# Ten weight slots, TensorE's expert pairs written out, and fillers ahead of a router's ranks

## The reference, cut to what matters

```python
xt = rmsnorm_2(x, norm2_g).reshape(T, D)                     # T = 512, D = 1024
g_logits = xt @ w_rg + b_rg;  g_idx = argmax(g_logits)       # 4 groups
e_in = (xt @ w_re + b_re).reshape(T, 4, 8)[group g_idx]      # 8 experts of the group
top_v, top_i = top_k(e_in, 2)
top_w = softmax(top_v) * softmax(g_logits)[g_idx]
# for each expert e, on the tokens xb that chose it:
ys = (silu(xb @ w_gate[e]) * (xb @ w_up[e])) @ w_down[e]     # 1024 -> 512 -> 1024
y[token] += top_w * ys
x = x + y
```

## Time and profile before

| | us |
|---|---|
| median of 3 runs | 1706.51 (1705.78 to 1707.2) |
| the profiled execution | 1707.3 |
| its span, first to last instruction | 1705.6 |
| TensorE busy in it | 1667.4 |
| VectorE busy | 807.9 |
| ScalarE busy | 321.3 |

### The profile page before, as it was taken

The page is one execution under the profiler, slowest core; times in us unless marked ns, Lnnn a source line. Parts: engine busy times, 40 slices in busy tenths (PEclk is TensorE's granted clock), DMA queues, the critical chain, the costliest instruction groups (busy, mean ns, idle before and its releaser), DMA issues.

```text
span 1705.6 us, 19789 instructions
## 1 busy us (share of the span) xinstructions
PE 1667.4 (98%) x7794; PEld 1044.1 (61%) x7794; DVE 807.9 (47%) x1762; ACT 321.3 (19%) x678; POOL 18.7 (1%) x39
## 2 busy tenths in 40 slices
PE   8999999999999999999999999999899999999998
PEld 4455544588888888878444455547754545454452
DVE  4973558587777772364895233335521211111123
ACT  1121334311111100120334244300200000000000
POOL 0001000000000000000000000000000000000001
PEclk9999999999999999999999999999999999999999
DMA  9976020012221213141211110533499999999998
GB/s 402 373 272 210 18 99 1 35 50 99 99 90 58 83 69 136 50 163 56 99 50 50 50 50 0 197 113 134 162 407 428 429 429 430 427 429 429 428 428 337
DMA packets 30247, 335.60 MB, mean 197 GB/s; under 512 B 3209, under 2 KB 5785, under 8 KB 10593
## 3 DMA queue, kind: packets, MB, share of 16 engines
q1 hardware_dynamic: 22464, 310.56, 44.7%
q10 hardware_dynamic: 5168, 14.91, 2.3%
q0 software_dynamic: 2544, 9.18, 1.5%
HBM read 319.66 MB, written 18.37 MB: 198 GB/s over the span
## 4 chain that ended last, share of the span: by engine, by line
PE 84%; DMA 7%; DVE 5%; ACT 2%; issue 1%; SPq 0%; ACTq 0%; DVEq 0%
PE bank L1497 16%; PE bank L1067 16%; PE bank L1115 8%; PE bank L1262 6%; PE bank L1506 5%; DMA pool<-in_w_expert_up 4%; PE bank L871 3%; PE bank L1270 3%; PE bank L1442 3%; PE bank L1184 3%; PE bank L1237 3%; PE bank L657 2%; DMA arena<-in_w_expert_up 2%; DMA pool<-in_w_ada 2%; PE bank L861 2%; PE bank L1039 2%
## 5 line engine op out<-in xcount | busy, mean ns | idle before, releaser
L1497 PE MATMUL bank<-pool,arena 128*64 128x512 f32 x1216 | 334.6, 594 | 7.3 <-DMA arena<-in_w_expert_up 3.8
L1067 PE MATMUL bank<-pool 128*128 128x256 f32 x1232 | 266.1, 379 | 0.8 <-ACT pool L2634 0.8
L1067 PEld LDWEIGHTS bank<-pool 128*128 128x128 f32 x1232 | 234.3, 190 | 32.4 <-issue 1.0
L1497 PEld LDWEIGHTS bank<-pool,arena 128*64 128x64 f32 x1216 | 107.6, 137 | 173.4 <-issue 164.3
L2550 DVE TENSOR_TENSOR arena<-arena,bank 128x512 f32<-128x512 f32 x16 | 11.0, 688 | 279.0 <-PE bank L1497 279.0
L1506 PEld LDWEIGHTS bank<-arena 128*128 128x128 f32 x960 | 109.5, 192 | 12.2 <-issue 12.2
L1262 PE MATMUL bank<-pool 128*128 128x512 f32 x256 | 114.5, 595 | 0.0
L1506 PE MATMUL bank<-arena 128*128 128x128 f32 x960 | 113.6, 277 | 0.0
L1262 PEld LDWEIGHTS bank<-pool 128*128 128x128 f32 x256 | 47.5, 190 | 55.3 <-issue 54.2
L1497 PE MATMUL bank<-xT,arena 128*64 128x512 f32 x160 | 70.6, 594 | 3.6 <-DMA pool<-in_w_expert_up 3.6
L1497 PE MATMUL bank<-arena 128*64 128x512 f32 x160 | 70.4, 593 | 0.0
(11 more groups left out here) (432 smaller groups left out, 2230.4 us busy)
## 6 DMA issues: line engine op xcount, KB each, us to landing
pool<-in_w_expert_gate SPq DMA_DIRECT2D x27, 2048.0 KB, 25.7
pool<-in_w_expert_down SPq DMA_DIRECT2D x27, 2048.0 KB, 28.0
pool<-in_w_expert_up SPq DMA_DIRECT2D x22, 2048.0 KB, 25.0
pool<-in_w_in SPq DMA_DIRECT2D x15, 2048.0 KB, 8.5
pool<-in_w_ada SPq DMA_DIRECT2D x12, 2048.0 KB, 18.8
pool<-in_w_up SPq DMA_DIRECT2D x11, 2048.0 KB, 8.1
arena<-in_w_expert_gate SPq DMA_DIRECT2D x5, 2048.0 KB, 29.8
xT<-in_w_expert_up SPq DMA_DIRECT2D x5, 2048.0 KB, 24.8
```

What stands on the lines that cost most here:

```text
L1067: ins = pe.matmul(up_quarter(u, p), lhs[:, k, :], rhs[:, k, :], start=(k == 0), stop=(k == 3))
L1497: ins = pe.matmul(dst[b * CAP:(b + 1) * CAP, :], lhs(b, k), rhs(b, k), start=(k == 0), stop=(k == n_k - 1))
```

## The change

- **A tenth slot.** `arena[:, 12800:16896]` becomes slot 9. Slab 9 (up of expert 3) is loaded into it once the first rows are transposed (`xk_full` at 1), ahead of `ring8` in SyncE's list. Slab c goes to slot c modulo 10; the use of slab c releases the load of slab c + 10. SyncE's list is a loop of two rounds over 30 loads and 26 loads written out: 86 in all, where there were 87.
- **Room for it.** The router's tables leave that part of `arena`: they go to 11264 to 12800, into `block1` and into `mn`. The squares get eight buffers in the new slot's place. `wpick` becomes `pick`, and `wpT` becomes `pickb`; so the weighted picks are made behind pair 14 instead of ahead of it.
- **TensorE's pairs** 1 to 15 are written out, with no loop.
- **Overflow blocks** on all four engines: block 0, then a `Fori` from 1 with an `If` inside.
- **Fillers**: `kept_warm(8, 5)` behind the transposes 0 to 5 and ahead of the wait for `oh_rdy`.
- Two semaphores used once each on ScalarE (`cact_rdy`, `e1_rdy`) become one, `ac_first`.

```diff
-        sqr = [view(arena, (11776, 12288, 12800, 15936, 12288, 12800, 15936, 12288)[m], T) for m in range(KD)]
+        sqr = [view(arena, 12800 + m * T, T) for m in range(KD)]
-        wpick = view(arena, 9728, NT, P)
-        pickO = (view(arena, 9728, NT, CAP), view(arena, 9984, NT, CAP))
-        xsO = view(arena, 15936, KD, CAP)
-        wpT = view(arena, 15936, NT, P)
+        wpick = pick
+        pickO = (view(arena, 8192, NT, CAP), view(arena, 8448, NT, CAP))
+        xsO = view(arena, 8704, KD, CAP)
+        wpT = pickb
-        xsT = view(arena, 10240, KD, P)
-        sg = view(arena, 11264, EF)
-        hE = view(arena, 11776, EF)
-        ysb = view(arena, 12288, D)
+        xsT = view(arena, 9728, KD, P)
+        sg = view(arena, 10752, EF)
+        hE = view(arena, 11264, EF)
+        ysb = view(arena, 11776, D)
-        ws += [arena[:, SLOT:2 * SLOT], hT.rearrange("p k t -> p (k t)"), xT.rearrange("p k t -> p (k t)")]
+        ws += [arena[:, SLOT:2 * SLOT], hT.rearrange("p k t -> p (k t)"), xT.rearrange("p k t -> p (k t)"), arena[:, 12800:16896]]
...
-        landed = [sem(f"landed{i}") for i in range(9)]
+        landed = [sem(f"landed{i}") for i in range(10)]
-        loads = [0] * 9
+        loads = [0] * 10
...
+
+        def tables(base, r_at, end, *shapes):
+            for name, shape in shapes:
+                R[name] = view(base, r_at, *shape)
+                r_at += int(np.prod(shape))
+            assert r_at <= end, r_at
+
+        tables(arena, 11264, 11776, ("t2", (2, NT * E)), ("cm", (E, 7)))
+        tables(arena, 11776, 12800, ("io", (E,)), ("r4", (4,)), ("g7", (7,)), ("bs", (E,)), ("ohs", (NT + 1, E)), ("lg", (NT, 36)),
+               ("gs", (NT, 4)), ("g1", (NT, 4)), ("gm", (NT,)), ("gx", (NT,)), ("em", (NT, E)), ("top", (NT, 8)), ("ix", (NT, 8)),
+               ("d", (NT,)), ("oh", (2, NT * E)), ("nb", (E,)), ("adj", (E,)), ("rk", (2, NT)), ("rb", (2, NT)), ("big", (2, NT)))
+        tables(block1, 0, P, ("cin", (E,)), ("be", (2, E)), ("bx", (2,)), ("ge", (NT, 4)), ("pg", (NT,)), ("w1", (NT,)), ("ed", (NT,)))
+        mn = sb("mn", [P, 2 * P])
+        tables(mn, 36, P, ("sl", (2, NT)), ("slo", (2, NT)))
+        tables(mn, P, 2 * P, ("row", (P,)))
...
-        turn9 = (0, 3, 1, 4, 2, 5, 6, 7, 8)
+        turn10 = (0, 3, 1, 4, 2, 5, 6, 7, 8, 9)
...
                 load(("eu", 1), 4, up_of(1))
+                load("ring9", 9, up_of(3), (S["xk_full"], 1))
                 load("ring8", 8, up_of(2), (S["xk_full"], 2 * NT))
                 sp.wait_ge(S["ov_step"], 1)
...
 
-                    used, of = ("g_full", "uu_full", "yy_full")[r % 6 // 2], (gate_of, up_of, down_of)[(r + 9) % 6 // 2]
-                    at = turn9[r % 9]
-                    sp.wait_ge(S[used], i * 3 + (r // 6 + 1))
-                    sp.dma_start(ws[at][:, :], of(i * 6 + (2 * ((r + 9) // 6) + (r + 9) % 2)))\
-                      .then_inc(landed[at], 16)
-
-                with sp.Fori(0, 4) as i:
-                    for r in range(18):
+                    used, of = ("g_full", "uu_full", "yy_full")[r % 6 // 2], (gate_of, up_of, down_of)[(r + 10) % 6 // 2]
+                    at = turn10[r % 10]
+                    sp.wait_ge(S[used], i * 5 + (r // 6 + 1))
+                    sp.dma_start(ws[at][:, :], of(i * 10 + (2 * ((r + 10) // 6) + r % 2))).then_inc(landed[at], 16)
+
+                with sp.Fori(0, 2) as i:
+                    for r in range(30):
                         next_slab(i, r)
-                for r in range(15):
-                    next_slab(4, r)
+                for r in range(26):
+                    next_slab(2, r)
                 for t in range(NT):
                     sp.wait_ge(S["comb"], LAST.index((t, 1)) + 1)
...
                     rows_of(x)
+                kept_warm(8, 5)
                 pe.wait_ge(S["oh_rdy"], 1)
                 pe.matmul(bank[3][:, 0:(NT + 1) * E], tris[:, :], R["ohs"].rearrange("p t e -> p (t e)"), start=True, stop=False)
                 for t in range(NT):
...
-                base += [16] * 3
+                base += [16] * 4
 
                 def placed(i, c):
 
-                    at = turn9[c % 9]
-                    return at, i * 32 + (base[at] + 16 * (c // 9))
+                    at = turn10[c % 10]
+                    return at, i * 48 + (base[at] + 16 * (c // 10))
 
                 def both_k(n_k, lhs, rhs, dst, later=None):
 
...
-                def block_of(i, n_more, least):
-
-                    with pe.If(n_more > least):
-                        pe.wait_ge(S["ov_step"], i * OVS + 2)
-                        if i == 0:
-                            n_more = pe.value_load(smi[0:1, 42:43], min_val=0, max_val=OVB)
-                            pe.wait_ge(S["xt_ev"], 2)
...
-                        ins.then_inc(S["ov_step"], 1)
-                        if i + 1 < OVB:
-                            block_of(i + 1, n_more, i + 1)
-                        if i == 0:
-                            pe.wait_ge(S["ov_back"], 48)
-
-                block_of(0, most, CAP)
+                def block_of(i):
+
+                    pe.wait_ge(S["ov_step"], i * OVS + 2)
+                    if isinstance(i, int):
+                        pe.wait_ge(S["xt_ev"], 2)
+                    for k in range(KD):
...
+                    for half in range(2):
+                        ins = full_k(0, lambda k: hET[:, k, 0:CAP], lambda k: w[:, k, half * 512:(half + 1) * 512], n_k=4,
+                                     sl=bank[6 + half][0:CAP, :])
+                    ins.then_inc(S["ov_step"], 1)
+
+                with pe.If(most > CAP):
+                    block_of(0)
+                    n_more = pe.value_load(smi[0:1, 42:43], min_val=0, max_val=OVB)
+                    with pe.Fori(1, OVB) as i:
+                        with pe.If(n_more > i):
+                            block_of(i)
+                    pe.wait_ge(S["ov_back"], 48)
                 pair(0, [placed(0, c) for c in range(6)], first=True)
-                with pe.Fori(0, 4) as i:
-                    for q in range(1, 4):
-                        pair(i * 3 + q, [placed(i, 6 * q + c) for c in range(6)])
-                for p in range(13, E // 2):
+                for p in range(1, E // 2):
                     pair(p, [placed(0, 6 * p + c) for c in range(6)], last=(p == E // 2 - 1))
 
                 pe.wait_ge(S["xt_ev"], E + 1)
...
 
-                def picks(i, weighted=False):
-
+                def picks(i, last=False):
 
...
                     ve.tensor_tensor(pick, pick, pickb, ALU.add).then_inc(S["pick_rdy"], 1)
-                    if weighted:
-                        ve.wait_ge(S["pick_rdy"], i + NT)
-                        for t in range(NT):
-                            for b, dst_ in enumerate((wpick, pickb)):
-                                ins = ve.tensor_scalar(dst_[:, t, :], R["row"], R["sl"][:, b, t:t + 1], wt[:, b, t:t + 1],
-                                                       ALU.is_equal, ALU.mult)
-                        ins.then_inc(S["pick_part"], 1)
-                        ve.wait_ge(S["pick_part"], i * 2 + 1)
-                        ve.tensor_tensor(wpick, wpick, pickb, ALU.add).then_inc(S["pick_rdy"], 1)
+                    if last:
                         return
                     ve.tensor_scalar(R["sl"], R["sl"], float(-P), None, ALU.add).then_inc(S["pick_part"], 1)
                     ve.wait_ge(S["pick_part"], i * 2 + 1)
                     ve.wait_ge(S["pick_rdy"], i + NT)
+
+                def weights_placed(i):
+
+                    ve.wait_ge(S["pick_rdy"], i + NT)
+                    for t in range(NT):
+                        for b, dst_ in enumerate((wpick, pickb)):
+                            ins = ve.tensor_scalar(dst_[:, t, :], R["row"], R["sl"][:, b, t:t + 1], wt[:, b, t:t + 1],
+                                                   ALU.is_equal, ALU.mult)
+                    ins.then_inc(S["pick_part"], 1)
+                    ve.wait_ge(S["pick_part"], i * 2 + 1)
+                    ve.tensor_tensor(wpick, wpick, pickb, ALU.add).then_inc(S["pick_rdy"], 1)
 
             if on("end"):
                 n2 = col("norm2", 0, 8)
...
                     pair(p, False, False)
                     picks(p + 2)
                 pair(E // 2 - 3, False, False)
-                picks(E // 2 - 1, weighted=True)
+                picks(E // 2 - 1, last=True)
                 pair(E // 2 - 2, False, False)
+                weights_placed(E // 2 - 1)
                 pair(E // 2 - 1, False, True)
                 ve.wait_ge(gath[0], 64)
                 for t in range(2):
```

More of the change, by code:

```diff
@@ L408, in two_blocks @@
         rs1 = view(upper, 7168, 512)
-        mn = sb("mn", [P, 2 * P])
         mnf, mnb = mn[:, 0:P], mn[:, P:2 * P]
@@ L1601, in _ @@
-                block_of(0, most, CAP)
+                def block_of(i):
[4 more added lines that the diff above has]
+                        for t in range(NT):
```

(45 more changed lines are left out.)

123 lines of the change are left out of this document (35 added, 88 removed).

## The result

The changed kernel takes 1710.36 us (median of 9 runs, 1707.74 to 1712.11), beside 1706.62 for the kernel before in the same comparison (9 runs, 1705.29 to 1708.79): a ratio of 1.0019, 95% interval 1.0010 to 1.0028. Forecast were 1699.5 and a range up to 1702.6. It is slower, by 0.2%, where 0.4% faster was forecast. The profiled execution took 1711.37 us, 4.1 more than its counterpart of before.

The account below looks back on a forecast made before the run. TensorE and DMA were both taken as at their limit, DMA pacing the last pairs. Slot -5.1, fillers -2.4 and fetches +0.5 made -7.0 us, from a median of 1706.5 to 1699.5; range 1697.0 to 1702.6.

Parts of the forecast that it names:

- The jump over the overflow blocks: TensorE's jump ahead of pair 0, over two blocks instead of fifteen: nothing, bounds a gain of 1.2 and a loss of 1.5.
- One more such gap: Loss bound of the jump ahead of pair 0: another idle gap of TensorE like the present one, 1.5 us.
- The fetches of the written-out pairs: Expert stage: 13 instruction fetches of 16 KB added to a full DMA stream, 0.5 us lost by bytes.
- The rival with one DMA engine: Expert stage: one of 16 DMA engines carries all added fetches, 7.9 us instead of 0.5, time 1706.9; chance 0.05.
- The row taken against it: Chain of waits before the change: pairs 10 to 12 without a fetch take 61.12 us, 12 to 14 with two 61.18.
- The tenth slot: Expert stage: each awaited slab lands one place earlier in the DMA stream, 5.1 us gained, bounds 4.9 and 6.1.
- The fillers: Router, ahead of the ranks: eight fillers keep TensorE's clock at full, so the expert stage starts 2.4 us earlier.
- The loop's jump back: TensorE's loop over pairs, between pairs 3 and 4: costs nothing, 28.53 us across it, so writing out saves nothing there.
- slot, clock, fetches, jump: The forecast's bounds: slot 4.9 to 6.1, clock (by the fillers) 1.8 to 2.9, fetches 0.4 to 1, jump either way.

Follow-up runs that it names:

- c_early: c_fixed with the tenth slot's slab requested as the router works, ahead of ring8: 1705.08 us, ratio 0.9994 to the kernel before.
- c_fixed: Changed kernel's layout and fillers, loops of the kernel before; tenth slot filled once, with slab 78, behind pair 0's first matmul: 1701.81 us, ratio 0.9968.
- a_late9: Changed kernel with slab 9 requested when pair 0's first matmul has run, not as the router works: 1703.73 us, ratio 0.9985.
- b_flat: Kernel before with only TensorE's pairs 1 to 15 written out, nine slots, no fillers: 1711.07 us, ratio 1.0026.
- c_nofill: c_fixed without the eight fillers: 1702.47 us, ratio 0.9975 to the kernel before.
- b_fill: Kernel before with only the eight fillers added ahead of the wait for the ranks' input: 1705.87 us, ratio 0.9993.
- a_nofill: Changed kernel without the eight fillers ahead of the ranks: 1709.39 us, ratio 1.0011 to the kernel before.
- a_late9_loop5: a_late9 with TensorE's pairs 1 to 10 as two rounds of a five-pair loop, 11 to 15 written out: 1704.49 us, ratio 0.9986.

## Why the prediction was wrong

**The jump over the overflow blocks** is the step that failed first. It was priced at nothing, with a loss of at most 1.5, although the text named what happens: ring8 and ring9 in flight when the target is fetched. It measured 5.7 us at the start of pair 0 (2.7 of gap, 3.0 of matmuls at the lower level behind it). c_early against c_fixed shows it with one load moved, a_late9 against the changed kernel as well; and that the code is what TensorE waits for is shown by the instruction packet, 1.52 to 1.61 us ahead of pair 0 in every kernel and late only where the tenth slot's slab is in flight. "One more such gap" was the wrong bound: the packet is as late as the slabs take to drain, and the clock comes on top. The text's own numbers could have priced it. By an estimate from them, four slabs at 4.89 us, the first issued at 1203.52, are in the queues until 1223.1 at the earliest, and the gathering ahead of the jump was forecast to end at 1222.4. The text asked of the fourth slab only whether it delays the first reload, at 1233.61.

**The fetches of the written-out pairs** are the second. Priced at 0.5 by bytes, they measured 4.5 us in b_flat (14.7 against 10.2 lost; 3.2 of a later slab, 1.3 of clock behind it) and 4.3 us in the median. The rival with one DMA engine (7.9) had the right mechanism, slabs land with the slowest engine, and the wrong distribution: the distance of the first engine from the last grows from 2.3 to 5.7 us. Its price was low besides: a packet takes about 1.0 us of its engine and not 0.61 (five were 0.3% of 16 engines over 105 us). That the setbacks fall on several engines is an estimate: twelve of 1.0 us on one would be 12 us, and the distance grew by 3.3. Which engine took which fetch isn't shown. The row taken against it, 61.18 against 61.12 us, had two fetches in it, and those may fall on engines that are ahead. Two of thirteen was no sample.

**The tenth slot** did what the text said. The cleanest comparison is c_nofill with the kernel before, both with the loop of three pairs and without fillers: 6.2 us lost against 10.2, and 3.9 us in the medians, for a slab worth 4.1 there. b_flat loses 14.7 us, a_late9, which adds the slot, 9.6: 5.1 less, as priced, though the two differ in more than the slot. The changed kernel has 11.1 lost where 5.1 were forecast: 4.5 are the fetches, and the other 1.5 are more of the same, since the slab that pair 14 awaits is 6.8 us from first to last write there, 5.5 in a_late9, and lands 1.3 us later, counted from pair 0's mark. Why the engines are further apart than in a_late9 stays open.

**The fillers** gave 2.1 us of the 2.4 in the profile. In the medians they are worth 0.9 (b_fill) and 0.7 (c_nofill to c_fixed), neither clear of nothing; and in the changed kernel nothing is left of them at the mark of pair 0, and the median without them (a_nofill) is 1.0 lower. The hole ahead of the ranks is not the only place where the clock falls.

**The loop's jump back** at nothing held for the body of three pairs. The rule of the Trainium skill ("Runtime: NRT & Kernel Launch", section on instruction fetch), that a taken branch stalls when its target isn't in the current window of two pages, is not borne out there: the body of three pairs ran on without a packet or a stall. At the body of five pairs (2.4 us) and at the jump over the overflow blocks the trace agrees with it.

**The range.** The bounds given with it (slot, clock, fetches, jump), taken all at once, make 1696.7 to 1702.3 and not 1697.2 to 1701.5. The measured time is outside both, so this isn't the step that failed.

The gain forecast was thus made, by 5.1 of the slot and 2.1 of the fillers, and given back twice, 5.7 at the jump and 4.5 by the fetches: 3.0 us slower. With the other 1.5 at pair 14's slab, 0.3 ahead of the router and -0.6 in the tail these are the 4.1 between the two profiled executions, to 0.1; the medians differ by 3.7.

## What to carry to other kernels

When DMA bounds the end of a stage, code is one of its transfers: writing a loop out adds fetches to a full stream, and a jump out of the fetched code should fall where the queues are empty. A prefetch can cost more than it saves by being early; ask which unseen transfer it stands ahead of. And a transfer that is spread over many engines lands with the slowest, so a small disturbance is priced by the worst engine and not by its bytes.

## What the runs showed of the hardware that was not expected

- With 16 DMA engines busy, 11 or 12 extra fetches of 16 KB (0.2 MB beside 113) left the rate at 428 GB/s, where it was 429, and widened the engines' finish of a slab from 2.3 to over 5 us.
- At the jump TensorE went on 1.52 to 1.61 us after the end of the last 16 KB instruction packet, in twelve kernels; the packet started up to 1.9 us behind the gathering's end where a slab stood ahead of it, and 0.9 to 1.2 us before it where none did.
- A body of three pairs ran four times with no instruction packet from its second round on; a body of five was fetched again, with 2.4 us at the jump.
- No length of a wait divides the cases in which the granted clock falls. In the twelve kernels, from the mark of pair 0 to that of pair 14, it fell behind ten waits of 1.98 to 3.6 us and stayed at 1.00 behind seven of 1.99 to 3.1 us (a_late9_loop5: 1.00 over the half behind 3.12 us; c_early: 0.81 behind 1.98 us and 1.00 behind 2.17 us); behind shorter ones it never fell. Each fall cost 1.3 to 1.7 us of the half behind it. So long waits risk more than short ones of the same sum.
